# A sparse mixer on one core: latents and expansion weights split for three single-pass products, another order of the indexer, relevance on row halves

## The chip, the cores and the metric

The kernel runs on one core of one Trainium2 chip. The metric is the time of one execution on the device, in microseconds (us); the lower the better. TensorE (PE) multiplies, VectorE (DVE) and ScalarE (ACT) read its results out of PSUM and prepare its operands, GpSimd (POOL) computes the factors of the norms, and SyncE (SP) issues the transfers.

## The reference

A decoder trunk of two layers over 256 tokens of width 1024. Each layer is a half-step FFN, a token mixer, a cross-attention to a memory, and a second half-step FFN, each with a norm before and after. The mixer of the second layer is sparse, and it alone is changed:

```python
def dsa_mixer(h, w_in, cq_g, ckv_g, w_uq, w_uk, w_uv):
    cq, ckv, qi, ki, wi = jnp.split(h @ w_in, C_SPLITS, axis=-1)      # 384, 256, 512, 64, 8
    q = (rmsnorm(cq, cq_g) @ w_uq).reshape(b, s, C_HEADS, C_NOPE)     # 8 heads of 128
    ckv = rmsnorm(ckv, ckv_g)
    ...
        rel = jax.nn.relu(jnp.einsum('bthd,bsd->bths', qi[:, i0:end], ki[:, :end]))
        score = jnp.einsum('bths,bth->bts', rel, wi[:, i0:end]).astype(jnp.float32)
        _, idx = lax.top_k(jnp.where(admissible, score, -jnp.inf), kk)   # kk = 64
        ...
        p = jax.nn.softmax(jnp.where(valid[:, :, None, :], logits, -jnp.inf), -1)
```

Queries, keys and values of the 8 heads are expanded from two normalised latents (`cq`, 384 wide, and `ckv`, 256 wide). An indexer of 8 heads of 64 scores every earlier token, and attention sees only the 64 best of each query. Queries are done in two blocks of 128 tokens (t = 0 and 1).

## The kernel before

All five engines run one written-out program, each its own instructions in order; the order is written by hand in one block per engine, and semaphores tie the engines together. The sub-layers follow each other: FFN 3, FFN 4 (the FFN ahead of the sparse mixer), the mixer (number 5), cross-attention 6, FFN 7.

**Products.** Almost every weight goes through a split. SP loads a chunk of up to 128x2048 f32 into one of two `raw` buffers, ACT rounds it to fp32r in the ring `w_ring` (`hi_half`, L1656), and DVE subtracts to get the rest (`lo_half`, L2322). Activations are split in the same way, and a product is done as three single-pass matmuls, high by high, high by low and low by high (`token_terms`, `feature_terms`, `three_products`). `split_to(c)` in the ACT and DVE blocks is the place at which these engines split the chunks up to `c`; SP loads a chunk into a `raw` buffer once the low half of the chunk two before it is done. The ring has four places; a chunk is split into its place when the chunk four before it has had its last use.

The sparse mixer has chunks that are not split: `ca` and `cb` hold the expansion weights of queries (`cuq`), keys (`cuk`) and values (`cuv`) in plain f32, and `latT` holds the transposed latents in plain f32. `up` (L1298) multiplies them. A plain f32 matmul stands in the trace as two records.

**Names in the mixer.** `relevance(t, i)`: qi by ki for two heads of query block t; each of its two matmuls takes the two heads together (128 rows) against keys that are zero in one half of the rows (`kk2`, `kiT`). On ACT it is a ReLU out of PSUM, on DVE two multiply-adds into `score` (tensor `vaug`, L2756). `top_rounds`: rounds of MAX8 and MATCH_REPLACE8, eight for each block; `top_mask` makes the mask out of them. `queries(p)`, `keys(p)`: expansion for heads 2p and 2p+1. `latent_values(i, t)`: values of four heads and one block. `sparse_scores(n)`, on DVE `row_max` (mask, row maximum; its first instruction frees the PSUM bank), on ACT `exps`, on DVE `normalise` (which gives `prob_done`), on PE `prob_transposes`, on ACT `prob_copy`, on PE `sparse_values`, on ACT `output_hi`, on DVE `output_lo` (which frees the bank): this is the way of one pair of heads, units us[0] to us[3] for block 0 and us[4] to us[7] for block 1.

**PSUM banks.** Four banks rotate over results in the order of the string `SPARSE`; PE may write result n only when the engine that reads result n-4 has freed it.

## Time and profile before

| | |
|---|---|
| runs, us | 1086.25, 1084.6, 1086.06; median 1086.06 |
| profiled execution, us | 1085.41, of which the span of instructions is 1083.7 |
| granted TensorE clock, mean | 0.999 |
| PE busy | 1070.7 us, 99% of the span |
| DVE busy | 776.0 us, 72% |
| ACT busy | 564.6 us, 52% |
| chain that ended last | PE 91%, DVE 5%, ACT 2% |

Times in the rows are us from the start of the span. A row of the timeline gives start, duration, engine, line and operation; equal instructions in sequence are one row with their count, and the duration of a PE row includes the draining of its last matmul, so that the pace of PE is read from start to next start. The sparse mixer runs from 748.10 to 846.39.

### The profile page before, as it was taken

The numbers are of one execution on the slowest core, as the hardware profiler recorded it, in microseconds if no ns is written. First come the engines' busy times: TensorE is split into PE (matmuls) and PEld (weight loads), VectorE is DVE, ScalarE is ACT, GpSimd is POOL, SyncE is SP. The second block draws the span as 40 slices with busy tenths as digits, with TensorE's granted clock in tenths as the row PEclk, the third lists the DMA queues.
The fourth block names the chain that finished last, engine by engine and source line by source line (L and its number), as shares of the span: only waits on it lengthen the run. The fifth ranks groups of instructions, "written<-read, shape, count | busy, mean of one in ns | idle before, by whom it ended". The sixth has DMA issues, their size and how long they took to land.

```text
span 1083.7 us, 16043 instructions
## 1 busy us (share of the span) xinstructions
PE 1070.7 (99%) x6172; PEld 938.9 (87%) x6172; DVE 776.0 (72%) x1015; ACT 564.6 (52%) x816; POOL 67.8 (6%) x169
## 2 busy tenths in 40 slices
PE   8999999999999999999999999999999999999997
PEld 7888888998889888888888888888978989888886
DVE  5966769875886786676778667678487768676675
ACT  6534446667766753443465344345466666443442
POOL 3000010110020200000010000002100101000000
PEclk9999999999999999999999999999999999999999
DMA  8756474564144365644536564453804435745641
GB/s 322 249 192 222 165 273 132 170 205 151 50 184 152 108 247 199 228 166 183 194 108 246 209 233 159 190 194 108 272 14 143 175 117 195 252 159 191 222 165 40
DMA packets 50155, 194.59 MB, mean 180 GB/s; under 512 B 4496, under 2 KB 24480, under 8 KB 31792
## 3 DMA queue, kind: packets, MB, share of 16 engines
q1 hardware_dynamic: 48832, 189.54, 49.2%
q0 software_dynamic: 1264, 4.25, 1.4%
q8 instruction: 38, 0.62, 0.2%
q14 instruction: 21, 0.17, 0.0%
HBM read 192.73 MB, written 1.05 MB: 179 GB/s over the span
## 4 chain that ended last, share of the span: by engine, by line
PE 91%; DVE 5%; ACT 2%; issue 1%; DMA 1%; POOL 0%; SPq 0%; POOLq 0%; ACTq 0%; DVEq 0%
PE psum L960 21%; PE psum L1076 21%; PE psum L968 11%; PE psum L941 5%; PE psum L1061 3%; PE psum L1298 3%; PE psum L946 3%; PE psum L784 2%; PE psum L786 2%; PE psum L785 2%; PE psum L980 1%; PE psum L1267 1%; PE psum L1168 1%; PE psum L810 1%; PE psum L811 1%; PE psum L809 1%
## 5 line engine op out<-in xcount | busy, mean ns | idle before, releaser
L2322 DVE TENSOR_TENSOR w_ring<-raw,w_ring 128x2048 fp32r<-128x2048 f32 (+2 forms) x120 | 272.8, 2273 | 25.4 <-ACT w_ring L1656 25.1
L1656 ACT ACTIVATE w_ring<-raw 128x2048 fp32r<-128x2048 f32 x121 | 230.7, 1907 | 47.3 <-DMA raw<-in_ffn_w_gate 25.3
L2439 DVE TENSOR_REDUCE work<-psum 128x256 f32<-128x512 f32 x172 | 114.4, 687 | 175.3 <-PE psum L968 161.2
L960 PE MATMUL psum<-h_both,w_ring 128*128 128x512 f32 x1024 | 237.3, 389 | 0.0
L960 PEld LDWEIGHTS psum<-h_both,w_ring 128*128 128x128 f32 x1024 | 192.2, 188 | 39.9
L1076 PE MATMUL psum<-w_ring,g_both 128*128 128x512 f32 x936 | 220.0, 390 | 0.0
L1076 PEld LDWEIGHTS psum<-w_ring,g_both 128*128 128x128 f32 x936 | 173.2, 188 | 34.3
L1754 ACT ACTIVATE V<-work 128x512 f32<-128x512 f32 x44 | 27.9, 634 | 249.3 <-DVE work L2448 249.3
L968 PEld LDWEIGHTS psum<-h_both,w_ring 128*128 128x128 f32 x1024 | 127.1, 192 | 2.5
L968 PE MATMUL psum<-h_both,w_ring 128*128 128x256 f32 x1024 | 127.9, 283 | 0.0
L2322 DVE TENSOR_TENSOR w_ring<-QT,w_ring 128x2048 fp32r<-128x2048 f32 x40 | 91.4, 2285 | 2.4 <-ACT w_ring L1656 2.4
L1656 ACT ACTIVATE w_ring<-QT 128x2048 fp32r<-128x2048 f32 x40 | 76.2, 1905 | 1.9 <-DMA QT<-in_ffn_w_down 1.9
L1758 ACT ACTIVATE g_both<-V 128x512 fp32r<-128x512 f32 x43 | 27.2, 633 | 73.7 <-DVE V L2455 73.7
L941 PE MATMUL psum<-h_both,w_ring 128*128 128x512 f32 x240 | 57.7, 393 | 0.0
L941 PEld LDWEIGHTS psum<-h_both,w_ring 128*128 128x128 f32 x240 | 44.3, 188 | 8.8
L784 PE MATMUL psum<-h_both,w_ring 128*128 128x256 f32 x128 | 36.6, 286 | 0.9 <-DVE work L2559 0.9
L1688 ACT ACTIVATE h_both<-psum,gcol 128x128 fp32r<-128x128 f32 x112 | 30.8, 385 | 12.0 <-PE psum L1168 12.0
L786 PE MATMUL psum<-h_both,w_ring 128*128 128x256 f32 x128 | 36.2, 283 | 0.0
L785 PE MATMUL psum<-h_both,w_ring 128*128 128x256 f32 x128 | 36.2, 283 | 0.0
L1076 PE MATMUL psum<-w_ring,h_both 128*128 128x512 f32 x144 | 34.9, 396 | 0.0
L2455 DVE TENSOR_TENSOR V<-V,work 128x512 f32<-128x512 f32 x43 | 29.8, 692 | 6.3 <-ACT V L1754 2.8
L2354 DVE SCALAR_TENSOR_TENSOR h_both<-psum,gcol,h_both 128x128 fp32r<-128x128 f32 x112 | 30.3, 343 | 4.6 <-ACT h_both L1688 4.0
(336 smaller groups left out, 1560.7 us busy)
## 6 DMA issues: line engine op xcount, KB each, us to landing
raw<-in_ffn_w_gate SPq DMA_DIRECT2D x43, 1024.0 KB, 4.8
raw<-in_ffn_w_up SPq DMA_DIRECT2D x43, 1024.0 KB, 4.8
QT<-in_ffn_w_down SPq DMA_DIRECT2D x40, 1024.0 KB, 4.8
raw<-in_ab_w_in SPq DMA_DIRECT2D x7, 1024.0 KB, 5.5
gain_row<-in_norm_g POOLq DMA_DIRECT2D x8, 512.0 KB, 6.6
raw<-in_ffn_w_down SPq DMA_DIRECT2D x4, 1024.0 KB, 4.7
raw<-in_xa_wk SPq DMA_DIRECT2D x4, 1024.0 KB, 4.8
raw<-in_ab_w_out SPq DMA_DIRECT2D x4, 1024.0 KB, 5.0
```

The lines of the kernel that those rows point to most:

```text
L784: nc.tensor.matmul(o, wh, a_hi[:, k, :], start=(k == 0), stop=False)
L785: nc.tensor.matmul(o, wh, a_lo[:, k, :], start=False, stop=False)
L786: last = nc.tensor.matmul(o, wl, a_hi[:, k, :], start=False, stop=(k == KT - 1))
L941: nc.tensor.matmul(outs[j][:, :], hi[:, k, P * j:P * (j + 1)], h_both[:, k].rearrange("p a n -> p (a n)"), start=(k == 0), stop=False)
L946: last = nc.tensor.matmul(outs[j][:, 0:TOK], lo[:, k, P * j:P * (j + 1)], h_hi[:, k, :], start=False, stop=(k == KT - 1))
L960: nc.tensor.matmul(outs[-1][:, :], hi[:, k, P * j:P * (j + 1)], h_both[:, k].rearrange("p a n -> p (a n)"), start=(k == 0), stop=False)
L968: last = nc.tensor.matmul(outs[2 * n + j][:, 0:TOK], lo[:, k, P * j:P * (j + 1)], h_hi[:, k, :], start=False, stop=(k == KT - 1))
L1061: last = nc.tensor.matmul(psum[:, 2 * t + half, :], a, w[:, k, 512 * half:512 * (half + 1)], start=(first and k == 0 and a is ah and w is hi),
L1076: last = nc.tensor.matmul(psum[:, 2 * t + half, :], a, w[:, k, 512 * half:512 * (half + 1)], start=(first and k == 0 and a is ah and w is hi),
L1656: nc.scalar.activation(w_hi[:, c % RING, 0:k * n], raw_at(c)[:, 0:k * n], ACT.Copy)\
L2322: nc.vector.tensor_tensor(w_lo[:, c % RING, 0:k * n], raw_at(c)[:, 0:k * n], w_hi[:, c % RING, 0:k * n].bitcast(F32), ALU.subtract).then_i ...
L2439: nc.vector.tensor_reduce(dst[:, p % 2, TOK * j:TOK * (j + 1)], bank(name).rearrange("p (a n) -> p n a", a=2), AX.X, ALU.add)\
```

## The change

The two unsplit chunks are gone. `cuq.0`, `cuk`, `cuv` and `cuq.1` (1536, 2048, 2048 and 1536 columns) become ordinary chunks that ACT and DVE split; the latents are split too: ACT writes `lat_hi` and DVE writes `query_lo` and `key_lo` (`latent_lo`). Queries, keys and values are computed by `three_products`. The column groups of the input projection are regrouped, so that what the indexer and the queries need comes first and the latent of keys and values (`c.1`) last, in two steps, one for each block. `relevance` multiplies 64 rows by 64 rows, one head in the upper and one in the lower half of the array, each half into a PSUM bank of its own. The order of the whole mixer is written anew.

```diff
-    add("ca", *uq, uk[0], split=False)
-    add("cb", uk[1], *uv, split=False)
+    add("cuq.0", uq[0])
+    add("cuk", uk)
+    add("cuv", uv)
+    add("cuq.1", uq[1])
...
-C_COLS = [("c.0", (0, 256)), ("c.1", (256, 512)), ("c.2", (512, 640), (1152, 1224)), ("qi.0", (640, 896)),
-          ("qi.1", (896, 1152))]
+C_COLS = [("c.2", (256, 384), (1152, 1224)), ("c.0", (0, 256)), ("qi.0", (640, 896)), ("qi.1", (896, 1152)),
+          ("c.1", (384, 640))]
...
 SPARSE = """
-    rel0.0 rel0.1 rel1.0 rel1.1 ccqT.0 ccqT.1 cckvT rel0.2 rel0.3 cuq.0.0 rel1.2 rel1.3 cuk.0 cuq.0.1
-    score{0} cuk.1 cuv.0.0 score{1} cuq.1.0 pT{0} cuk.2 cuv.1.0 pv{0} score{2} pT{1} cuq.1.1 cuk.3 pv{1} cuv.0.1
+    rel0.0 rel0.1 c.1.0 rel0.2 rel0.3 c.1.1 rel1.0 rel1.1 cuq.0.0 cckvT rel1.2 rel1.3 cuq.0.1 cuk.0 cuk.1
+    cuv.0.0 cuv.1.0 score{0} score{1} cuk.2 pT{0} cuq.1.0 pv{0} score{2} pT{1} cuk.3 cuq.1.1 pv{1} cuv.0.1
     score{3} pT{2} cuv.1.1 pv{2} score{4} pT{3} pv{3} score{5} pT{4} score{6} pv{4} pT{5} score{7} pv{5} pT{6}
...
-            def relevance(t, i):
+            def relevance(t, m):
                 n = P * (t + 1)
-                up(f"rel{t}.{i}", [(slice(TOK * j, TOK * j + n),
-                                    [(qiT[:, i, P * t:P * (t + 1)], kiT[:, j, 0:n])]) for j in range(2)])
+                outs = [take(f"rel{t}.{2 * m + j}") for j in range(2)]
+                for i in range(2):
+                    for j in range(2):
+                        o = slice(64 * j, 64 * (j + 1))
+                        last = nc.tensor.matmul(outs[j][:, TOK * i:TOK * i + n], qiT[o, 2 * m + i, P * t:P * (t + 1)],
+                                                kiT[o, 0, 0:n], start=True, stop=True)
...
             def keys(p):
-                w = resident(f"cuk_{p // 2}").rearrange("p (h k) n -> p h k n", h=4)
-                up(f"cuk.{p}", [(slice(TOK * j, TOK * (j + 1)),
-                                 [(w[:, 2 * (p % 2) + j, k, :], latT[:, 3 + k, :]) for k in range(2)])
-                                for j in range(2)])
+                w = weights(C["cuk"])
+                three_products(f"cuk.{p}", [(slice(TOK * j, TOK * (j + 1)),
+                                             [([a[:, 2 * (2 * p + j) + n, :] for a in w], key_latent(n))
+                                              for n in range(2)]) for j in range(2)])
...
 # PE, order
-            relevance(0, 2)
-            relevance(0, 3)
             ready("ccqT.0")
             ready("ccqT.1")
             queries(0)
-            relevance(1, 2)
-            relevance(1, 3)
+            pe.wait_ge(lat_done, 4)
+            transposes("cckvT", [lat[:, t, QL + P * k:QL + P * (k + 1)] for k in (0, 1) for t in range(NT)])
+            relevance(1, 1)
+            queries(1)
             ready("cckvT")
             keys(0)
-            queries(1)
-            sparse_scores(0)
             keys(1)
             latent_values(0, 0)
+            latent_values(1, 0)
+            sparse_scores(0)
             sparse_scores(1)
+            keys(2)
+            prob_transposes(us[0])
             queries(2)
-            prob_transposes(us[0])
-            keys(2)
-            latent_values(1, 0)
             sparse_values(0)
             sparse_scores(2)
             prob_transposes(us[1])
+            keys(3)
             queries(3)
-            keys(3)
             sparse_values(1)
             latent_values(0, 1)
             sparse_scores(3)
...
 # DVE, order
-            for t, i in RELEVANCE:
-                relevance(t, i)
-            top_rounds(0, range(rounds))
+            latent_lo("ccqT.0", query_lo, 0, 2, 4)
+            latent_lo("ccqT.1", query_lo, 2, 1, 5)
+            split_to(C["cuq.0"])
+            relevance(0, 0)
+            relevance(0, 1)
+            split_to(C["cuk"])
+            relevance(0, 2)
+            relevance(0, 3)
+            split_to(C["cuv"])
+            latent("cckv", QL, QL + KVL)
+            top_rounds(0, range(2))
+            relevance(1, 0)
+            relevance(1, 1)
+            latent_lo("cckvT", key_lo, 0, 2, 6)
+            top_rounds(0, range(2, rounds))
             top_mask(0)
             row_max(us[0])
+            relevance(1, 2)
+            relevance(1, 3)
+            split_to(C["cuq.1"])
             top_rounds(1, range(0, 2))
+            top_rounds(1, range(2, 4))
             normalise(us[0])
             row_max(us[1])
-            top_rounds(1, range(2, 4))
+            top_rounds(1, range(4, 6))
             normalise(us[1])
-            top_rounds(1, range(4, 6))
+            top_rounds(1, range(6, rounds))
+            top_mask(1)
             row_max(us[2])
             output_lo(us[0])
-            top_rounds(1, range(6, rounds))
             normalise(us[2])
             split_to(C["co.0"])
             output_lo(us[1])
-            top_mask(1)
             row_max(us[3])
```

The place on which most depends is DVE between the row maximum of the first pair of heads and its normalised probabilities. Before, on DVE (`work<-psum,xmT` and `nmax<-work` are `row_max`, `einv` and `work<-work,einv` are `normalise`):

```order
L2559 SCALAR_TENSOR_TENSOR work<-psum,xmT 128x2x128 [waits bank_full1,dve_chain]
L2562 TENSOR_REDUCE nmax<-work 128x2 [waits bank_read1]
L2766 MAX top<-vaug 128x8
L2767 MATCH_REPLACE vaug<-top,vaug 128x256 [waits dve_chain]
L2766 MAX top<-vaug 128x8 [waits dve_chain]
L2767 MATCH_REPLACE vaug<-top,vaug 128x256 [waits dve_chain]
L2567 RECIPROCAL einv<-esum 128x2 [waits exp_done,dve_chain]
L2574 TENSOR_TENSOR work<-work,einv 128x2x128 [waits dve_chain]
```

In the changed kernel the same stretch of DVE begins so (the pair of rows MAX and MATCH_REPLACE follows four times before the RECIPROCAL, where it stood twice):

```order
L2593 SCALAR_TENSOR_TENSOR work<-psum,xmT 128x2x128 [waits bank_full1,dve_chain]
L2596 TENSOR_REDUCE nmax<-work 128x2 [waits bank_read1]
L2799 SCALAR_TENSOR_TENSOR vaug<-shared,iw,vaug 128x256 [waits bank_read2]
L2799 SCALAR_TENSOR_TENSOR vaug<-shared,iw,vaug 128x256 [waits dve_chain]
L2799 SCALAR_TENSOR_TENSOR vaug<-shared,iw,vaug 128x256 [waits bank_read3,rel_used]
L2799 SCALAR_TENSOR_TENSOR vaug<-shared,iw,vaug 128x256 [waits dve_chain]
L2356 TENSOR_TENSOR w_ring<-raw,w_ring 128x1536 [waits split_hi,rel_used]
L2809 MAX top<-vaug 128x8
L2810 MATCH_REPLACE vaug<-top,vaug 128x256 [waits dve_chain]
```

Four multiply-adds of the relevance, the low half of chunk `cuq.1` and two more rounds now stand between `row_max` and `normalise`.

The other place is PE ahead of the transposes of the first probabilities, the rows that wait for `prob_done`. Before (`KTs,QT` is `sparse_scores(1)`, the six `latT,w_raw` are `queries(2)`):

```order
L1267 MATMUL psum<-KTs,QT 128x128 [waits bank_read0,bank_read2]
L1267 MATMUL psum<-KTs,QT 128x128
L1298 MATMUL psum<-latT,w_raw 128x256 [waits bank_read1,resident_full_ca]
L1298 MATMUL psum<-latT,w_raw 128x256 x5
L1153 MATMUL psum<-ident,work 128x128 [waits bank_read2,prob_done]
L1153 MATMUL psum<-ident,work 128x128
```

In the changed kernel the end of that stretch on PE (the last three of the twelve products of `keys(2)`, the transposes, the first three of `queries(2)`):

```order
L1380 MATMUL psum<-lat_hi,w_ring 128x256
L1381 MATMUL psum<-key_lo,w_ring 128x256
L1382 MATMUL psum<-lat_hi,w_ring 128x256
L1159 MATMUL psum<-ident,work 128x128 [waits bank_read0,prob_done]
L1159 MATMUL psum<-ident,work 128x128
L1380 MATMUL psum<-lat_hi,w_ring 128x256 [waits bank_read1,split_lo]
L1381 MATMUL psum<-query_lo,w_ring 128x256
L1382 MATMUL psum<-lat_hi,w_ring 128x256
```

`queries(2)` has moved behind the transposes; between `sparse_scores(0)` and them PE now has `sparse_scores(1)` and `keys(2)` alone.

## Rows read from the trace of the kernel before

**Rows 1.** The page: its first line and part 1, busy us of PE.

```profile
span 1083.7 us, 16043 instructions
PE 1070.7 (99%) x6172; PEld 938.9 (87%) x6172; DVE 776.0 (72%) x1015; ACT 564.6 (52%) x816; POOL 67.8 (6%) x169
```

**Rows 2.** Windows of the mixer: stretch, length, busy us by engine, granted clock, DMA.

```profile
748.10:766.10 18.00, 18.00 (x152) 17.84 (x153) 12.60 (x21) 13.10 (x21) 4.56 (x8) 1.00 0.58 186
782.95:799.22 16.27, 15.97 (x75) 12.95 (x73) 12.29 (x45) 9.06 (x17) 0.00 (x0) 1.00 0.00 1
```

**Rows 3.** Timeline of PE in the sparse mixer: start, duration, line, operation.

```profile
780.77 1.25 PE L1153 MATMUL psum<-ident,lat 128*128 128x128 f32 x10
781.86 1.26 PE L1298 MATMUL psum<-krT,shared 128*128 128x128 f32 x8
782.95 2.76 PE L1298 MATMUL psum<-latT,w_raw 128*128 128x256 f32 x12
785.55 1.89 PE L1298 MATMUL psum<-krT,shared 128*128 128x256 f32 x8
787.27 4.48 PE L1298 MATMUL psum<-latT,w_raw 128*128 128x256 f32 x20
791.59 0.61 PE L1267 MATMUL psum<-KTs,QT 128*128 128x128 f32 x4
...
793.76 1.88 PE L1298 MATMUL psum<-w_raw,latT 128*128 128x512 f32 x4
795.48 0.61 PE L1267 MATMUL psum<-KTs,QT 128*128 128x128 f32 x4
796.36 2.83 PE L1298 MATMUL psum<-latT,w_raw 128*128 128x256 f32 x12 [0.27 <-DVE work L2559]
799.22 0.44 PE L1153 MATMUL psum<-ident,work 128*128 128x128 f32 x2
...
814.22 0.38 PE L1153 MATMUL psum<-ident,work 128*128 128x128 f32 x2
```

**Rows 4.** Timeline of PE in the first mixer, around `three_products`.

```profile
238.86 0.28 PE L1374 MATMUL psum<-lat_hi,w_ring 128*128 128x256 f32 x1
...
246.06 0.40 PE L1374 MATMUL psum<-w_ring,lat_hi 128*128 128x512 f32 x1
...
248.81 2.84 PE L1298 MATMUL psum<-w_raw,work 128*128 128x128 f32 x24
```

**Rows 5.** Timeline of DVE in the sparse mixer.

```profile
787.37 2.05 DVE L2756 SCALAR_TENSOR_TENSOR vaug<-shared,iw,vaug 128x256 f32<-128x256 f32 x4 [2.03 <-ACT shared L1669]
...
795.79 0.42 DVE L2559 SCALAR_TENSOR_TENSOR work<-psum,xmT 128x256 f32<-128x256 f32 x1
...
796.58 0.42 DVE L2766 MAX8 top<-vaug 128x8 f32<-128x256 f32 x1
...
798.54 0.17 DVE L2567 RECIPROCAL einv<-esum 128x2 f32<-128x2 f32 x1
...
799.08 0.42 DVE L2559 SCALAR_TENSOR_TENSOR work<-psum,xmT 128x256 f32<-128x256 f32 x1
...
807.96 2.28 DVE L2322 TENSOR_TENSOR w_ring<-raw,w_ring 128x2048 fp32r<-128x2048 f32 x1
810.16 0.42 DVE L2583 TENSOR_TENSOR h_both<-psum,h_both 128x256 fp32r<-128x256 f32 x1
...
811.27 0.42 DVE L2559 SCALAR_TENSOR_TENSOR work<-psum,xmT 128x256 f32<-128x256 f32 x1
```

**Rows 6.** Timeline of ACT: a split in the mixer.

```profile
807.33 1.90 ACT L1656 ACTIVATE w_ring<-raw 128x2048 fp32r<-128x2048 f32 x1
```

**Rows 7.** PE at the two ends of the span, and the last window's clock.

```profile
5.07 1.20 PE L903 MATMUL psum<-h_both,w_ring 128*128 128x512 f32 x2
...
1073.68 4.24 PE L1061 MATMUL psum<-w_ring,g_both 128*128 128x512 f32 x18
...
1081.50:1082.00 0.50, 0.00 (x0) 0.00 (x0) 0.00 (x0) 0.00 (x0) 0.00 (x0) 0.50 1.03 381
```

More of the change, by code:

```diff
@@ L1520, in _, with key_value_latent @@
             relevance(0, 0)
+            def key_value_latent(t):
+                hi, lo = weights(C["c.1"])
+                filled(f"c.1.{t}", token_terms(take(f"c.1.{t}")[:, 0:256], hi, lo, h_hi, h_lo, t))
+            key_value_latent(0)
+            ready("qi.1")
             relevance(0, 1)
-            filled("qi.1", feature_terms(out_[:, TOK:2 * TOK], hi, lo, h_hi, h_lo, 1))
+            key_value_latent(1)
             relevance(1, 0)
-            relevance(1, 1)
-            pe.wait_ge(lat_done, 3)
@@ new lines, in key_latent @@
+            def key_latent(n, o=slice(0, TOK)):
+                return lat_hi[:, 3 + n, o], key_lo[:, n, o]
+            def queries(p):
+                w = weights(C[f"cuq.{p // 2}"])
+                heads = [slice(HD * h, HD * (h + 1)) for h in (2 * (p % 2), 2 * (p % 2) + 1)]
+                three_products(f"cuq.{p // 2}.{p % 2}", [(slice(TOK * j, TOK * (j + 1)),
+                                                          [([a[:, n, heads[j]] for a in w], query_latent(n))
+                                                           for n in range(3)]) for j in range(2)])
@@ L1544, in latent_values @@
             def latent_values(i, t):
-                w = resident(f"cuv_{i}").rearrange("p (h k) n -> p h k n", h=4)
-                up(f"cuv.{i}.{t}", [(slice(0, 512), [(tile(latT[:, 3 + k, :], t), w[:, :, k, :]) for k in range(2)])])
+                w = [a.rearrange("p (h k) n -> p h k n", k=2)[:, 4 * i:4 * i + 4] for a in weights(C["cuv"])]
+                three_products(f"cuv.{i}.{t}", [(slice(0, 512), [(key_latent(n, slice(P * t, P * (t + 1))),
+                                                                  [a[:, :, n, :] for a in w]) for n in range(2)])])
@@ L2092, in _ @@
             us = units_of("dsa")
[L2093 to L2094 removed]
             queries(0)
+            latent_rows("cckvT", 3, 2)
             relevance(1, 2)
             relevance(1, 3)
+            queries(1)
+            split_to(C["cuq.1"])
             keys(0)
[L2099 to L2108 removed]
+            keys(1)
+            latent_values(0, 0)
+            latent_values(1, 0)
+            exps(us[0])
+            exps(us[1])
+            keys(2)
+            prob_copy(us[0])
+            queries(2)
+            split_to(C["co.0"])
             output_hi(us[0])
@@ L2744, in _, with latent @@
             dve.wait_ge(ki_done, 1)
-            for name, a, b in (("ccq", 0, QL), ("cckv", QL, QL + KVL)):
+            def latent(name, a, b):
                 for t in range(NT):
@@ L2748, in _, with latent_lo @@
                 ins.then_inc(lat_done, 1)
-            split_to(C["qi.1"] + 2)
+            split_to(C["qi.1"])
+            latent("ccq", 0, QL)
+            split_to(C["c.1"])
+            def latent_lo(name, dst, k, n, done):
+                dve.wait_ge(lat_hi_done, done)
+                first = k if dst is query_lo else 3
+                for j in range(n):
+                    ins = nc.vector.scalar_tensor_tensor(dst[:, k + j, :], bank(name)[:, TOK * j:TOK * (j + 1)],
+                                                         pcol[:, CCQ + first + j:CCQ + first + j + 1],
+                                                         lat_hi[:, first + j, :].bitcast(F32), ALU.mult, ALU.subtract)
+                ins.then_inc(freed[name][0], 1)
             def relevance(t, i):
```

120 lines of the change are left out of this document (58 added, 62 removed).

## The prediction

> **What bounds the kernel now.** I read the page first: PE is busy for 99% of a span of 1083.7 us [rows 1]. Then the windows of the sparse mixer: PE is busy for all of the 18.00 us of the input projection and for 15.97 of 16.27 us where queries, keys and values are expanded, at clock 1.00, while DVE is busy for 12.29 and ACT for 9.06 of the latter [rows 2]. Then the timeline of PE through the mixer: its rows follow each other without a gap, and the only wait above 0.2 us is 0.27 us [rows 3]. So PE sets the pace before. What is taken from PE counts in full, as long as DVE and ACT keep up; the question is whether they do once they have more to do.
>
> **What the change takes from PE.** A plain f32 matmul of 256 columns costs 4.32/10 = 0.432 us (20 records, two a matmul, from 787.27 to 791.59), one of 512 columns 1.72/2 = 0.86 us [rows 3]. The kernel has the new form already in its first mixer: 60 single products of 256 columns from 238.86 to 246.06 are 0.120 us each, 12 of 512 columns up to 248.81 are 0.229 us each [rows 4]. Three of them are 0.36 and 0.69 us.
> - Queries and keys are 24 + 16 matmuls: 40 x 0.072 = 2.9 us less. Values are 8: 8 x 0.17 = 1.4 us less.
> - The transposes for `kiT` are 2 in place of 4: 2 x 0.11 (ten took 1.09 us [rows 3]) = 0.2 us less.
> - Relevance: the pair of calls for block 0 costs 1.09 us, for block 1 1.72 us [rows 3], twice each: 5.6 us. The changed kernel issues the same 16 matmuls over the same columns, with 64 rows of the array in place of 128. No row of before shows such a matmul. If the two halves of the array take turns, it costs 5.6 us as now (full); if they overlap wholly, 2.8 us (half). The nearest rows are the full-height ones, but consecutive matmuls go to different halves and banks, so I take the middle, 4.2 us (1.4 less), and keep both ends for the range.
>
> The Trainium skill bears on this term: "TensorEngine Tiling (Array Packing)", section Key Properties, has it that tiles on different rows load weights and multiply in parallel, and that a change of tiling mode drains the array. By that page the term would be near 2.8 us, and the sum below about 1 us lower. No row here shows it.
>
> Together PE has 2.9 + 1.4 + 0.2 + 1.4 = 5.9 us less to do. The regrouping of the input projection changes nothing for PE: the same 1.00-clock 18.00 us of columns, part of them later.
>
> **What it adds elsewhere.** DVE gets four low halves, two of 2048 and two of 1536 columns. One of 2048 is 2.20 us from start to next start (807.96 to 810.16 [rows 5]); scaled by columns one of 1536 is 1.7 (an estimate), so 7.8 us in all. Five low halves of latents of 256 columns from PSUM are 0.34 to 0.42 us each like the instruction at 810.16, 1.9 us. ACT gets four high halves, about 1.8 + 1.8 + 1.4 + 1.4 = 6.4 us by [rows 6]. SP has four more loads through the two `raw` buffers; each is issued when the low half two chunks before is done, 7 us or more before PE wants the product, so I cost them at nothing. Up to `cuv` all of this falls where DVE and ACT have idle time. The last of it does not, and this is the term that decides.
>
> **The wait that appears.** A timetable from the rows. PE starts the mixer at 748.10 as before. Until the first scores it now has: 18.00 (projection), 11.54 for the two halves of qi (two stretches of 48 single products of 0.12), 0.2 (`kiT`), 1.1 (ten latent transposes), 4.2 (all of relevance), 36 products of `queries(0)` and `(1)` 4.3, 24 of `keys(0)` and `(1)` 2.9, 12 of 512 columns for values 2.75, and the scores 0.44 (791.59 to 792.03, four records). That is 45.4 us; with 0.3 us that `keys(0)` waits for `key_lo`, the scores of us[0] are done at 793.8, and readable at about 794.0. DVE has then finished the eight rounds of block 0 and waits for them.
>
> From there DVE has, in its fixed order: `row_max` 0.79 (795.79 to 796.58), four multiply-adds of 256 columns 2.05, the low half of `cuq.1` 1.7, four rounds of 0.98 (two took from 796.58 to 798.54) 3.9, `normalise` 0.6 (798.54 to 799.08, and the end of the instruction) [rows 5]. Sum 9.0: `prob_done` comes at 803.0. PE in the meantime has 0.44 for `sparse_scores(1)` and 12 x 0.12 = 1.44 for `keys(2)`, and stands still from 795.7 to 803.0, **7.3 us**. Before, the transposes that wait for it started at 799.22 [rows 3]. They are 3.8 us late. Behind them on PE stand `queries(2)` and all that follows; no engine can go around.
>
> What is late next: PE then has 0.2 (transposes), 2.16 (`queries(2)`), 0.44 + 0.44 + 0.21, 1.44 (`keys(3)`), and would start `queries(3)` at 808.0. It goes to the bank of pv of us[0], which `output_lo(us[0])` frees. DVE comes to that after `row_max(us[1])` 0.79, two rounds 1.96, `normalise` 0.54, two rounds 1.96, the mask of block 1 0.8, `row_max(us[2])` 0.79 and its own 0.42: 7.3 us after 803.0, at 810.3. That is a second wait, **2.3 us**. A third: `latent_values(1, 1)` goes to the bank of us[1]'s pv. ACT frees the way only after it has evacuated `queries(3)` (812.5, and 0.6 for 512 columns, an estimate a little above a quarter of the 1.90 of 2048 [rows 6]), split `co.1` (1.8) and written the high half of 256 (0.4, estimated alike), then DVE 0.4: 815.8, while PE would be there at 814.9: **0.9 us**. The transposes of us[3] then start at 815.8 + 1.37 + 0.44 + 0.87 = 818.5, against 814.22 before [rows 3]: 4.3 us late. From there on both kernels have the same work, PE was without gaps before, and nothing gives it back: 4.3 us is the loss at the end too. As a check by sums: waits 0.3 + 7.3 + 2.3 + 0.9 = 10.8, less the 0.27 of before, less the 5.9 saved, is 4.6.
>
> **The clock.** PE never stood still for 7 us before. At the end of the span its last matmul ends at 1077.92, and the granted clock of 1081.5 to 1082.0 is 0.50, the lower level of 1.2 GHz [rows 7]. At the start, two products of 512 columns take 1.20 us with their draining (0.5 us each from start to start), twice the 0.229 of [rows 4, 7]. So I expect the clock to fall inside the 7.3 us, and some matmuls after it at half pace. If this holds for 5 us, PE reaches `queries(3)` at 810.5 in place of 808.0, which the second wait hides; but `sparse_scores(2)` comes at 809.7, just when DVE wants it, and up to 1 us gets through. I take 0.4, bounds 0 and 1.5. The skill's "TensorE: Matmul & The Clock Gate", Part 1, has the same: an idle engine falls to half clock and regains it only after sustained work. The trace's two ends agree with it.
>
> **Sum.** The profiled execution took 1085.41 us. + 4.3 + 0.4 = **1090.1 us**. That execution is 0.65 us below the median of the runs shown, so I put the forecast between the two bases, at 1090.4.
>
> **Rivals.**
> - *The added vector work is hidden* (faster). The whole 5.9 us would be kept and the time be 1079.5. For it speaks that DVE is idle for 4 of 16.27 us at the expansion [rows 2] and more before. It decides at one point: `normalise(us[0])` would have to end by 795.7, when PE is through with `keys(2)`. Against it: 9.0 us of DVE instructions stand between the scores and it, each with a row and all on one in-order engine, and PE cannot give the scores 7 us earlier. Chance 0.05.
> - *The loss and the gain nearly cancel* (within 2 us). With relevance at half, and the two bank waits absorbed because the instructions between are shorter out of PSUM than I have them, the loss would be 4.3 - 1.0 - 2.0 = 1.3: 1086.7. The first wait alone, 7.3, is already above the 5.9. Chance 0.09.
> - *The half clock lasts.* The page on the clock gate would allow that the second and third wait keep PE at 1.2 GHz. As a mechanism of this kernel: the PE work between 803 and 818, some 12 us, would take 12 us more, less the 3.2 us of waits that it fills: 8 us or more on top, 1098. Against it: the one fall that the trace shows comes after PE has stood still from 1077.92 until past 1081 [rows 7]; the later waits are 2.3 and 0.9 us. Chance 0.06.
> - *Relevance at full price or dearer* (drains between halves): 5.6 us or more, the scores 1.4 later, and so all behind: 1091.8. Chance 0.16.
> - The forecast as summed: chance 0.64.
>
> **Numbers.** 0.2% of 1086 us, about 2.2 us, is what a measurement of this kernel tells from no change. Slower by more: 0.64 + 0.16 + 0.06 and a part of the second rival, 0.87. Within: 0.08. Faster: 0.05. The range for 8 in 10 reaches from relevance at half, no clock term and the lower base (1085.4 + 3.3, less the 1 us by which single runs differ) to the full price with 1.5 us of clock on the median: 1087.7 to 1093.3.
>
> **What would show it.** In the changed kernel's trace: `prob_transposes` of us[0] with an idle time of about 7 us before it, put down to the DVE line of `normalise`; `queries(3)` with about 2 us; products of queries at 0.12 us each; relevance from PE's starts, 2.8 or 5.6 us in all; a window below 1.00 clock right after the first wait; the end of the mixer (846.39 before) at 850.5 to 851.5, and from there the same distance to the end. I am wrong if DVE's order leaves `normalise(us[0])` earlier than 801, if the loads of `cuk` or `cuv` come late (then PE waits before 787), or if PE shows gaps of its own at the change from one form of matmul to the other.

## The result and the profile after

The changed kernel takes 1092.82 us (median of 6 runs, 1091.66 to 1095.09), the kernel before in the same session 1086.07 us (6 runs). The ratio is 1.0062, 95% interval 1.0051 to 1.0074: it is slower by 6.75 us. The forecast was 1090.4 (1087.7 to 1093.3), so the sign and the range hold, and the time is 2.4 us above the forecast. The profiled execution took 1092.22 us.

The page of the changed kernel, its first line, busy us of each engine, and the chain that ended last [rows 1 for before]:

```profile
span 1090.5 us, 16158 instructions
PE 1068.2 (98%) x6218; PEld 939.4 (86%) x6218; DVE 786.1 (72%) x1023; ACT 570.6 (52%) x821; POOL 71.7 (7%) x169
PE 85%; DVE 7%; ACT 3%; DMA 3%; issue 1%; POOL 1%; SPq 0%; POOLq 0%; DVEq 0%; ACTq 0%
```

PE has 2.5 us less busy time in a span that is 6.8 us longer: it must stand still more. To compare executions whose sub-layers start at slightly different times, I measure the mixer from the second group of input transposes, inside its start, to the first group of the next sub-layer. The timeline of PE before:

```profile
751.09 1.18 PE L1168 MATMUL psum<-ident,x_state 128*128 128x128 f32 x8
...
844.13 1.04 PE L1168 MATMUL psum<-ident,x_state 128*128 128x128 f32 x8
```

That is 93.04 us. After, the same timeline with the rows that answer to [rows 3]:

```profile
751.35 1.28 PE L1174 MATMUL psum<-ident,x_state 128*128 128x128 f32 x8
...
773.39 0.71 PE L1521 MATMUL psum<-krT,shared 64*128 64x128 f32 x8
...
777.10 0.71 PE L1521 MATMUL psum<-krT,shared 64*128 64x128 f32 x8
...
780.82 1.14 PE L1521 MATMUL psum<-krT,shared 64*128 64x256 f32 x8
...
784.87 0.66 PE L1159 MATMUL psum<-ident,lat 128*128 128x128 f32 x4 [0.57 <-DVE lat L2379]
785.46 1.13 PE L1521 MATMUL psum<-krT,shared 64*128 64x256 f32 x8
...
789.26 0.36 PE L1380 MATMUL psum<-lat_hi,w_ring 128*128 128x256 f32 x1 [0.34 <-DVE key_lo L2789]
...
794.95 1.05 PE L1273 MATMUL psum<-KTs,QT 128*128 128x128 f32 x8
...
804.82 0.69 PE L1159 MATMUL psum<-ident,work 128*128 128x128 f32 x2 [7.38 <-DVE work L2608]
...
805.94 0.41 PE L1380 MATMUL psum<-lat_hi,w_ring 128*128 128x256 f32 x1
806.15 0.41 PE L1381 MATMUL psum<-query_lo,w_ring 128*128 128x256 f32 x1
...
809.14 1.05 PE L1295 MATMUL psum<-work,V 128*128 128x128 f32 x4
810.03 0.86 PE L1273 MATMUL psum<-KTs,QT 128*128 128x128 f32 x4
...
812.26 0.28 PE L1382 MATMUL psum<-lat_hi,w_ring 128*128 128x256 f32 x1
812.65 0.35 PE L1380 MATMUL psum<-lat_hi,w_ring 128*128 128x256 f32 x1
...
818.35 0.47 PE L1380 MATMUL psum<-w_ring,lat_hi 128*128 128x512 f32 x1 [0.81 <-DVE h_both L2617]
...
821.12 0.38 PE L1159 MATMUL psum<-ident,work 128*128 128x128 f32 x2
...
850.91 1.04 PE L1174 MATMUL psum<-ident,x_state 128*128 128x128 f32 x8
```

The mixer takes 850.91 - 751.35 = 99.56 us, 6.5 more than before, and that is the whole loss but for 0.2 us. What to see: a wait of 7.38 us before the transposes of us[0], put down to `normalise` (L2608); behind it products that start 0.21 us apart in place of 0.12; only a gap of some 0.3 us before `queries(3)` (812.65); 0.81 us before `latent_values(1, 1)`; and two small waits earlier (0.57 and 0.34). From 821.12 on both kernels go at the same pace, and nothing is given back.

Four windows of the same stretch (stretch, length, busy us of PE, PEld, DVE, ACT, POOL, granted clock, DMA):

```profile
796.00:800.00 4.00, 1.43 (x12) 1.23 (x11) 3.83 (x7) 1.93 (x5) 0.00 (x0) 1.00 0.00 0
800.00:804.00 4.00, 0.00 (x0) 0.00 (x0) 3.76 (x13) 0.00 (x0) 0.00 (x0) 0.52 0.65 204
804.00:808.00 4.00, 3.19 (x15) 3.19 (x16) 3.73 (x14) 1.63 (x6) 0.00 (x0) 0.50 0.15 60
808.00:812.00 4.00, 4.00 (x26) 3.87 (x25) 3.35 (x11) 2.62 (x4) 0.00 (x0) 0.70 0.02 4
```

PE is idle, DVE is full, ACT is idle, and the clock stands at 0.50, the level of 1.2 GHz, until about 810. DVE in this stretch:

```profile
795.67 0.42 DVE L2593 SCALAR_TENSOR_TENSOR work<-psum,xmT 128x256 f32<-128x256 f32 x1 [1.78 <-PE psum L1273]
...
796.46 2.04 DVE L2799 SCALAR_TENSOR_TENSOR vaug<-shared,iw,vaug 128x256 f32<-128x256 f32 x4
798.53 1.76 DVE L2356 TENSOR_TENSOR w_ring<-raw,w_ring 128x1536 fp32r<-128x1536 f32 x1
...
804.33 0.42 DVE L2608 TENSOR_TENSOR work<-work,einv 128x256 f32<-128x256 f32 x1
```

and ACT, its split of `cuq.1` and the end of the exponentials of us[0]:

```profile
789.46 1.48 ACT L1678 ACTIVATE w_ring<-raw 128x1536 fp32r<-128x1536 f32 x1
...
797.75 0.18 ACT L1846 ACTIVATION_READ_ACCUMULATOR work<-work,nmax 128x1 f32 x1
```

From `row_max` to the end of `normalise` DVE works for 9.1 us without a gap, while the exponentials that `normalise` needs were ready by 798. DVE was idle for 1.78 us right before, with the low half of `cuq.1` already possible (ACT had split it by 790.94).

### The profile page after: what moved, and what is told of

Its sections match the earlier page's. It is cut to its first block, busy times and chain, and to the rows that moved or that the text cites. A ratio compares the mean times of both kernels' runs of the same rounds, so it can differ in the third digit from the quotient of the medians.

```text
span 1090.5 us, 16158 instructions
## 1 busy us (share of the span) xinstructions
PE 1068.2 (98%) x6218; PEld 939.4 (86%) x6218; DVE 786.1 (72%) x1023; ACT 570.6 (52%) x821; POOL 71.7 (7%) x169
## 3 DMA queue, kind: packets, MB, share of 16 engines
HBM read 192.73 MB, written 1.05 MB: 178 GB/s over the span
## 4 chain that ended last, share of the span: by engine, by line
PE 85%; DVE 7%; ACT 3%; DMA 3%; issue 1%; POOL 1%; SPq 0%; POOLq 0%; DVEq 0%; ACTq 0%
PE psum L965 21%; PE psum L1082 21%; PE psum L973 11%; PE psum L946 5%; PE psum L1067 3%; PE psum L951 3%; DVE w_ring L2356 2%; PE psum L985 1%; ACT w_ring L1678 1%; PE psum L1273 1%; PE psum L789 1%; PE psum L791 1%; PE psum L790 1%; PE psum L1295 1%; DMA raw<-in_ab_w_in 1%
## 5 line engine op out<-in xcount | busy, mean ns | idle before, releaser
L2356 DVE TENSOR_TENSOR w_ring<-raw,w_ring 128x2048 fp32r<-128x2048 f32 (+2 forms) x124 | 280.8, 2265 | 24.7 <-ACT w_ring L1678 24.1
L1678 ACT ACTIVATE w_ring<-raw 128x2048 fp32r<-128x2048 f32 (+1 forms) x125 | 237.5, 1900 | 47.7 <-DMA raw<-in_ffn_w_gate 22.0
L681 POOL TENSOR_SCALAR part<-ss,eps_in 128x1 f32<-128x1 f32 x8 | 2.5, 312 | 476.5 <-ACT V L1700 476.5
```

The lines of the kernel that those rows point to most:

```text
L1678: nc.scalar.activation(w_hi[:, c % RING, 0:k * n], raw_at(c)[:, 0:k * n], ACT.Copy)\
L2356: nc.vector.tensor_tensor(w_lo[:, c % RING, 0:k * n], raw_at(c)[:, 0:k * n], w_hi[:, c % RING, 0:k * n].bitcast(F32), ALU.subtract).then_i ...
```

## The experiments

Theory A, my prediction's: PE saves 5.9 us, and DVE's order between the first scores and `normalise(us[0])` costs more than that. Rivals: the amount of new work on DVE and ACT, or late loads, or PE's new forms cost it. All ratios are to the kernel before, run beside each kernel. Mixer times are from one profiled execution each, and so can't give their own scatter; the medians also hold what varies ahead of the mixer, which in these executions starts (its second group of input transposes) anywhere between 750.80 and 753.50.

| kernel | median us | ratio, 95% interval | mixer us | first wait us |
|---|---|---|---|---|
| before | 1086.07 | | 93.04 | |
| changed | 1092.82 | 1.0062, 1.0051 to 1.0074 | 99.56 | 7.38 |
| DVE's order (e1_order) | 1087.73 | 1.0013, 1.0004 to 1.0022 | 94.96 | 2.80 |
| normalise first (e2_first) | 1094.38 | 1.0072, 1.0059 to 1.0084 | 100.90 | 3.45 |
| wait filled (e3_filler) | 1091.33 | 1.0054, 1.0041 to 1.0067 | 99.10 | 1.63 |
| relevance on full height (e4_rows) | 1092.80 | 1.0058, 1.0045 to 1.0071 | 99.82 | 7.38 |
| contiguous loads (e5_contig) | 1091.36 | 1.0052, 1.0036 to 1.0067 | 99.84 | 7.39 |
| DVE's order, wait half filled (e7_short) | 1087.24 | 1.0013, 1.0004 to 1.0023 | 93.07 | 1.36 |
| covered (e6_cover) | 1084.28 | 0.9990, 0.9981 to 0.9999 | 91.65 | 1.08 |
| covered, full height (e8_rows) | 1085.33 | 0.9997, 0.9987 to 1.0007 | 91.96 | 0.65 |
| covered, second version (e9_cover2) | 1083.80 | 0.9980, 0.9971 to 0.9989 | 90.80 | 1.09 |

**DVE's order alone.**

```diff
-            top_rounds(0, range(2, rounds))
+            top_rounds(0, range(2, 4))
+            relevance(1, 2)
+            top_rounds(0, range(4, 8))
+            relevance(1, 3)
             top_mask(0)
+            split_to(C["cuq.1"])
             row_max(us[0])
-            relevance(1, 2)
-            relevance(1, 3)
-            split_to(C["cuq.1"])
-            top_rounds(1, range(0, 4))
+            top_rounds(1, range(0, 1))
             normalise(us[0])
             row_max(us[1])
-            top_rounds(1, range(4, 6))
+            top_rounds(1, range(1, 3))
             normalise(us[1])
-            top_rounds(1, range(6, rounds))
-            top_mask(1)
-            row_max(us[2])
+            top_rounds(1, range(3, 5))
             output_lo(us[0])
+            row_max(us[2])
...
```

> The changed kernel with DVE's order alone rewritten inside the mixer: the low half of cuq.1 and the multiply-adds of relevance(1,2) and (1,3) go ahead of row_max(us[0]), where DVE is idle for 1.78 us, normalise(us[0]) stands one round after row_max(us[0]), output_lo(us[0]) ahead of row_max(us[2]), and the rounds of block 1 are spread up to row_max(us[4]). Theory A (the loss is DVE's order, which holds prob_done back): the 7.38 us before the transposes of us[0] fall to 1 to 3 us, the clock stays at 1.00, the mixer ends 6 to 7 us earlier, and the time is 1086 us (1084.5 to 1087.5). Theory B (the loss is in the new work itself, the amount that DVE and ACT have to do, or in PE's new forms): the wait moves to other places and the time stays at 1092 to 1093. Theory C (late loads of cuk and cuv set it): the same, 1092 or more.

Measured: 1087.73 us, 5.1 below the changed kernel, and the mixer 4.6 us shorter, though not one instruction of arithmetic was taken out. So the order, not the amount of work, made most of the loss; theories B and C fall as its main cause. But it is 1.7 us above what I expected, and 0.2 us above the upper end of my range. PE's timeline shows why:

```profile
802.18 0.44 PE L1159 MATMUL psum<-ident,work 128*128 128x128 f32 x2 [2.80 <-DVE work L2608]
802.37 0.36 PE L1380 MATMUL psum<-lat_hi,w_ring 128*128 128x256 f32 x1
...
802.69 0.41 PE L1382 MATMUL psum<-lat_hi,w_ring 128*128 128x256 f32 x1
802.89 0.42 PE L1380 MATMUL psum<-lat_hi,w_ring 128*128 128x256 f32 x1
```

The first wait is still 2.80 us, and after it the products go from 0.12 to 0.21 us apart, until 805.9: `queries(2)` takes 1.5 us more than at full clock. I had said that the clock would stay at 1.00. It did not: it stands at 1.00 from 802.40 to 802.60, when PE is at work again, and at 0.50 from 802.80 to 803.00. What is left of the wait is DVE's order too: the low half of `cuq.1` (797.94, 1.76 us) still stood ahead of `row_max(us[0])`, which began at 799.61. Its scores were there 2.0 us earlier, if they take as long to be read as in the changed kernel (794.95 to 795.67).

**`normalise(us[0])` ahead of the rounds, nothing else.**

```diff
             split_to(C["cuq.1"])
-            top_rounds(1, range(0, 2))
-            top_rounds(1, range(2, 4))
             normalise(us[0])
             row_max(us[1])
-            top_rounds(1, range(4, 6))
+            top_rounds(1, range(0, 6))
             normalise(us[1])
```

> The changed kernel with normalise(us[0]) and row_max(us[1]) moved ahead of the four rounds, nothing else. Theory A as a chain (all that stands on DVE up to row_max(us[2]) must be done, wherever normalise stands): the wait before the transposes of us[0] falls from 7.38 to about 3.5 us, and waits of together 3 to 4 us come up before the transposes of us[1] and queries(3); the time falls by the clock's share at most, 1091 to 1093. Rival (the first wait counts for itself, as my prediction summed it): 3.9 us less, about 1089.

Measured: 1094.38 us, not faster at all, and above the 1091 to 1093 that I gave it. The waits on PE:

```profile
801.49 0.44 PE L1159 MATMUL psum<-ident,work 128*128 128x128 f32 x2 [3.45 <-DVE work L2608]
808.70 0.44 PE L1159 MATMUL psum<-ident,work 128*128 128x128 f32 x2 [2.07 <-DVE work L2608]
812.66 0.55 PE L1380 MATMUL psum<-lat_hi,w_ring 128*128 128x256 f32 x1 [1.53 <-DVE h_both L2617]
```

The long wait halves, and two others come up, before the transposes of us[1] and before `queries(3)`. What counts is all that DVE has to do up to `row_max(us[2])` and `output_lo(us[0])`; a single wait is only where it shows. The mixer is even 1.3 us longer: with three waits in a row the granted clock stays low over five windows of 4 us from 800 (0.86, 0.71, 0.72, 0.50, 0.93), where the changed kernel had three. The rival of 1089 falls. That the clock makes up all of these 1.3 us was not tested.

**The wait filled with work on PE.**

```diff
-                for cols, terms in tiles:
+                for cols, terms in tiles * times:
...
-                                              for n in range(2)]) for j in range(2)])
+                                              for n in range(2)]) for j in range(2)], 5 if p == 2 else 1)
```

> The changed kernel, but PE does the twelve products of keys(2) five times into the same bank, which fills 5.8 of the 7.38 us wait with work and leaves the results as they are. Theory A1 (the half clock delays queries(2), ACT's split of co.0 behind it and so output_lo(us[0]) and queries(3)): no window below 1.00, queries(2) at 0.12 us a product, and the mixer ends 0.9 us earlier (0.6 to 1.3): 1091.9. Rival A2 (the second wait hides all of the half clock): no difference, 1092.8. Rival A3 (all of the half clock counts): 2.4 us less, 1090.4.

Measured: 1091.33 us, mixer 99.10, 0.46 us less than changed. The granted clock is 1.00 in every window from 796 to 820. From the transposes of us[0] to those of us[3] it takes 15.73 us (804.35 to 820.08), against 16.30 in the changed kernel (804.82 to 821.12), and the wait that the half clock had filled comes out:

```profile
804.35 0.44 PE L1159 MATMUL psum<-ident,work 128*128 128x128 f32 x2 [1.63 <-DVE work L2608]
811.61 0.36 PE L1380 MATMUL psum<-lat_hi,w_ring 128*128 128x256 f32 x1 [1.64 <-DVE h_both L2617]
```

So of some 2.7 us that the slow matmuls take more (`queries(2)` 3.99 for 2.16, values 0.89 for 0.44, scores 0.69 for 0.44, and the transposes), only 0.5 to 0.6 us reach the end. That is just below the lower end that I gave A1 (0.6 to 1.3) and not the nothing of A2; A3 (2.4 us) falls. The medians (1091.33 and 1092.82, from two sessions) have ratios with overlapping intervals and do not part A1 from A2.

**Relevance on the full height.**

```diff
-                        o = slice(64 * j, 64 * (j + 1))
-                        last = nc.tensor.matmul(..., qiT[o, 2 * m + i, ...], kiT[o, 0, 0:n], ...)
+                        last = nc.tensor.matmul(..., qiT[:, 2 * m + i, ...], kiT[:, j, 0:n], ...)
```

> The changed kernel with relevance on the full height again (the keys padded with zeros as before, kiT of four transposes, a memset on DVE), in the changed order. Theory A (PE sets the time at which the scores of us[0] are ready): relevance takes 5.6 in place of 3.4 us, less what it covers of the wait of 0.57 us before cckvT, plus 0.2 for the transposes: the scores and all behind are 1.9 to 2.4 us later, 1094.7 to 1095.2. Rival (DVE sets it, so that the row halves bring nothing): 1092.8. Rival (a change of form costs PE as much as the halves save): 1092.8 too, with relevance at about 5 us in the changed kernel's rows, which they don't show.

Measured: 1092.80 us, the same as changed; the mixer is 0.26 us longer. The 1.9 to 2.4 us of theory A were wrong twice. First, the price. The rows of this kernel:

```profile
783.28 1.89 PE L1520 MATMUL psum<-krT,shared 128*128 128x256 f32 x8
784.82 0.47 PE L1380 MATMUL psum<-lat_hi,w_ring 128*128 128x256 f32 x1
```

From its start to the next instruction a call of block 1 takes 1.54 us here and 1.06 in the changed kernel. That is not the whole, for the products behind it lose time too. Counted from the start of a call to that of the last product behind it, less 0.12 us for each product between, the four calls are 0.74, 0.75, 1.16 and 1.15 us in halves, with 0.09 or 0.10 lost ahead of each, and 0.88, 0.89, 1.72 and 1.72 on the full height, with next to nothing ahead: 4.2 against 5.2. (For the first: 773.39 to 776.89, 23 products further, is 3.50, less 23 x 0.12.) The halves save 1.0 us, with the two transposes 1.3. Second, of this only 0.3 arrives, because the waits of 0.57 and 0.34 us in the changed kernel disappear when PE comes later.

**Contiguous loads.** The two arrays are laid out so that a partition's part of `cuk` and `cuv` is one run.

```diff
+    elif name in ('c_w_uk', 'c_w_uv'):
+        a = a.reshape(a.shape[0], a.shape[1], 2, P, a.shape[3]).transpose(0, 3, 1, 2, 4)
```

> The changed kernel with c_w_uk and c_w_uv laid out in memory so that each partition's part of a chunk is one run of 8 KB in place of sixteen of 512 bytes; nothing else. Theory A (late loads make the wait before the transposes of cckvT): the two loads take 4.5 to 5 us from issue to landing, like the other loads of 1 MB, in place of 6.6 and 7.0; ACT's wait of 0.80 us before the split of cuk goes, and so does the wait of 0.57 us before the transposes of cckvT; the mixer, from the input transposes in it to those behind it, takes 99.0 us in place of 99.56. Rival (what DVE has to do sets the time of the key latent, with or without the loads): the wait of 0.57 stays, and the mixer with it.

The DMA issues of both kernels, the changed one first (median us from issue to landing; for the load in runs of 512 bytes the view gives the KB of a run, 0.5, not those of the whole):

```profile
raw<-in_c_w_uk SPq DMA_DIRECT2D x1, 0.5 KB, 6.6
raw<-in_c_w_uv SPq DMA_DIRECT2D x1, 0.5 KB, 7.0
```

```profile
raw<-in_c_w_uk SPq DMA_DIRECT2D x1, 1024.0 KB, 4.7
raw<-in_c_w_uv SPq DMA_DIRECT2D x1, 1024.0 KB, 4.8
```

As expected 2 us faster, and the wait before `cckvT` is gone: from the first relevance to the first scores it takes 20.79 us (774.60 to 795.39) in place of 21.56. The mixer as a whole does not show it in this execution: an earlier load of `c_w_in` landed later (the two loads took 6.1 us in the middle against 5.3), ACT waited for it for 3.28 us, and PE stood still for 0.98 us ahead of `qi.1`. That also brought PE to `cckvT` some 1.2 us later, which by itself would hide a wait of 0.57 us. The three kernels with these loads further down settle it: their PE is not late (first relevance at 772.88 to 773.23, against 773.39 in the changed kernel), and none has a wait before `cckvT` or for these loads. So the local effect is shown; in the total it is not told apart from nothing (ratio 1.0052 against 1.0062, intervals overlapping).

**The shorter wait, half filled.** The first of these kernels (DVE's order), with `keys(2)` done twice.

> The kernel of the first run (DVE's order alone rewritten), and PE does the products of keys(2) twice into the same bank: 1.44 us of work in the wait of 2.80 us that stood there. The clock had been below 1.00 after it (0.84 and 0.74 in two windows of 4 us). Theory A1 (a wait of 2.8 us is enough to lose the clock, one of 1.4 is not): no window below 1.00, and the mixer takes 94.0 us in place of 94.96. Rival (the half clock there was hidden by other waits): 94.9 as before.

Measured: the granted clock is 1.00 in all windows, and the mixer is 93.07, 1.9 us below 94.96, though PE does 1.44 us more. 0.3 us of this is a shorter wait before `cckvT`. The median fell only from 1087.73 to 1087.24 with the same ratio to before, so that the gain of 1 us and more stands in the two traces alone.

**The order that covers the softmax.** PE's part of the edit is shown. Four things differ from the changed kernel at once: the contiguous loads, PE's order, ACT's with it, and DVE's, which is not quite that of e1_order: `relevance(1, 3)` and `row_max(us[1])` stand between `row_max(us[0])` and `normalise(us[0])`, and the low half of `cuq.1` is done ahead of the last round of block 0. What each is worth was not measured apart.

```diff
             latent_values(0, 0)
-            latent_values(1, 0)
             sparse_scores(0)
+            latent_values(1, 0)
             sparse_scores(1)
             keys(2)
+            latent_values(0, 1)
             prob_transposes(us[0])
             queries(2)
...
             sparse_values(1)
-            latent_values(0, 1)
             sparse_scores(3)
+            latent_values(1, 1)
             prob_transposes(us[2])
-            latent_values(1, 1)
```

> Arithmetic, chunks and row halves of the changed kernel with the contiguous loads of the run before, DVE's order rewritten as in the first run, and PE's order (with ACT's and the banks') changed so that the time of us[0]'s softmax is covered: latent_values(1, 0) behind sparse_scores(0), latent_values(0, 1) behind keys(2), latent_values(1, 1) behind sparse_scores(3). Theory A (the new arithmetic is worth 5 us on PE, and only waits took it away): PE waits 2 to 4 us in all in the mixer, the clock stays at 1.00, the mixer takes 90 to 91.5 us against 93.04 before, and the time is 1083.5 us (1082.5 to 1085), below the kernel before. Rival (DVE has too much to do between the scores and row_max(us[4]), in any order): the waits go elsewhere and sum to over 6 us, and the time is not below 1086.

Measured: 1084.28 us, ratio 0.9990 (0.9981 to 0.9999), as expected; the mixer, 91.65, is 0.15 us above what I gave it. Its waits are 3.5 us in all, the longest of them is new, and the clock is 1.00:

```profile
811.50 0.68 PE L1293 MATMUL psum<-work,V 128*128 128x128 f32 x4 [1.32 <-ACT work L1689]
```

**The same with relevance on the full height.** The edit is that of the kernel with full height above.

> The kernel of the run e6_cover with relevance on the full height again (keys padded with zeros, kiT of four transposes). By the rows of the two kernels run so far relevance with the changes of form around it takes 5.4 us on the full height and 4.45 in halves, and two transposes take 0.27. Theory A (in the changed order the halves bring little only because waits behind them give way, and in a kernel without these waits they count): 1.0 to 1.3 us more than that kernel. Rival (they bring nothing anywhere): within 0.3 us of it.

Measured: mixer 91.96, 0.31 us more; by the traces theory A missed. The waits give way again: 0.32 us before `keys(0)` is gone, and 1.08 before the transposes of us[0] becomes 0.65. The medians are 1.05 us apart (1085.33 and 1084.28), which would fit theory A, but the intervals overlap, and they cannot decide between 0.3 and 1.

**The second version of the cover.** `latent_values(1, 1)` goes back behind the transposes of us[2], and `prob_copy(us[2])` ahead of `exps(us[3])` on ACT. DVE's order differs in some places too: the low half of `cuq.1` now stands behind `row_max(us[0])`, `relevance(1, 3)` behind `row_max(us[1])`.

> The kernel of the run e6_cover with latent_values(1, 1) back behind the transposes of us[2], prob_copy(us[2]) ahead of exps(us[3]) on ACT, and small moves in DVE's order. In e6_cover PE waited 1.32 us before the values of us[2], because the copy of their probabilities had nothing to hide behind. Theory A (that wait was the order's): it falls to 0.5 us or less, the mixer takes 90.5 to 91.2 us in place of 91.65, and the time is 1083.5 us (1082.5 to 1084.5). Rival (DVE is full from the scores to row_max(us[4]) and any cover only moves the wait): 91.5 to 92 us again.

Measured: 1083.80 us, ratio 0.9980 (0.9971 to 0.9989): faster than both kernels. The wait before the values of us[2] is 0.30 us and the mixer 90.80.

```profile
798.64 0.44 PE L1157 MATMUL psum<-ident,work 128*128 128x128 f32 x2 [1.09 <-DVE work L2606]
...
810.32 0.68 PE L1293 MATMUL psum<-work,V 128*128 128x128 f32 x4 [0.30 <-DVE h_both L2615]
```

The first wait, 1.09 us, is still in part order. The exponentials of us[0] are complete at 797.12, but DVE is at `relevance(1, 3)` then, and `normalise` begins at 797.96:

```profile
796.93 0.99 DVE L2797 SCALAR_TENSOR_TENSOR vaug<-shared,iw,vaug 128x256 f32<-128x256 f32 x2
797.96 0.17 DVE L2599 RECIPROCAL einv<-esum 128x2 f32<-128x2 f32 x1
```

In the same chain ACT spends 1.28 us (from 794.94) on loading its table ahead of the first exponential. Neither was tried out.

**Each matmul of relevance three times,** in halves and on the full height, to part the price of a matmul from that of the change of form.

```diff
-                for i in range(2):
+                for i in 3 * (0,) + 3 * (1,):
...
```

> The changed kernel with each matmul of relevance issued three times into the same place, so that what a matmul on half of the rows costs stands apart from what a change of form costs. Theory A (the halves overlap in part): by the changed kernel's rows, 1.06 us for a call of block 1 (four matmuls, eight records) and 0.64 for one of block 0, so the calls take 3.2 and 1.9 us. Theory B (they overlap wholly, and the rest is the cost of the change of form): every further repetition of block 1 costs 0.86 us, half of the 1.72 of the kernel before, and the call takes 2.8 us; block 0 1.6 us. Theory C (they do not overlap; the first figure only looks short because the next instruction shows later): 1.72 us for a repetition, 4.5 us for the call.

> The same threefold issue in the kernel e4_rows, relevance on the full height. A call of block 1 took 1.54 us there by its row and 1.82 with what the next products lose; a call of block 0 0.81 and 0.88. If a matmul on the full height costs what it did in the kernel before (0.43 us for 256 columns, 0.22 to 0.27 for 128), the calls take 5.0 to 5.2 and 2.6 to 3.0 us.

Each of the two kernels ran once (1096.17 and 1102.28 us); only their traces are used. PE in the two, halves first, with a call of block 0 and one of block 1:

```profile
778.05 1.61 PE L1522 MATMUL psum<-krT,shared 64*128 64x128 f32 x24
779.59 0.39 PE L814 MATMUL psum<-w_ring,h_both 128*128 128x256 f32 x1
...
782.66 2.86 PE L1522 MATMUL psum<-krT,shared 64*128 64x256 f32 x24
785.45 0.39 PE L1380 MATMUL psum<-lat_hi,w_ring 128*128 128x256 f32 x1
```

```profile
784.28 5.34 PE L1521 MATMUL psum<-krT,shared 128*128 128x256 f32 x24
789.27 0.47 PE L1380 MATMUL psum<-lat_hi,w_ring 128*128 128x256 f32 x1
```

A call of block 1 takes 2.79 us in halves, 1.73 more than once: 0.865 for each further issue. On the full height it takes 4.99 us, 3.45 more than once: 1.73 for each. The halves cost exactly half, as theory B has it: two of them run in the time of one matmul on the full height. That they do so side by side is the reading; a matmul on one half with none on the other was not run, so that 64 rows alone take half the time is not excluded. What a single call costs beyond this, with the 0.09 ahead of it, is 1.25 - 0.865 = 0.39 us for block 1 and 0.83 - 0.445 = 0.39 for block 0 (a further issue is 0.445 there: 1.54 us for the call of 778.05, 0.65 once). On the full height there is nothing beyond (1.72 against 1.73), in calls that stand between the same products; so I put the 0.4 us down to the change to halves and back.

## Why the prediction was right, and where it was short

The mechanism held: PE saved less than it then lost to a wait for `normalise(us[0])`, and DVE's order made that wait. Signs by which I would see it are there (7.38 us before the transposes of us[0], products at 0.12 us, a window below 1.00), except that the mixer ended at 853.17, not between 850.5 and 851.5, and `queries(3)` waited for 0.3 us, not for 2. Two of my three signs of being wrong came up as well, both small: the load of `cuk` came late, and PE has gaps where the form changes.

- **PE bound before, less on PE after: right, and the sum nearly so.** The waits in the rows sum to 9.1 us, but they are counted from the end of a drained matmul. From start to start, less the usual pace, PE loses 0.73, 0.49, 7.55, 0.27 and 1.06 us, 10.1 in all, and 2.7 by half pace: 99.56 - 12.8 = 86.8 us of work, against 93.04 - 0.6 = 92.4 before. So about 5.7 us were saved, forecast 5.9 (an estimate from these rows, good to some tenths). Products are 0.12 us apart as read from the first mixer.
- **Relevance: right in size by luck.** I took the middle between "the halves take turns" and "they overlap" (4.2 us), and it came to 4.2, but not by a middle of the two. The halves come at half the price, 2.6 us in all, and each of the four calls loses 0.39 us beside. The Trainium skill has both in "TensorEngine Tiling (Array Packing)", Key Properties: tiles work in parallel, and a change of mode drains the array; the runs agree, with 0.865 against 1.73 us and 0.39 us a call. My reading that the page gives 2.8 us left out the drains, whose size it does not state: 1.6 us in four calls, more than half of the 2.8 us that the halves give.
- **Loads at nothing: wrong by 0.6 to 0.7 us.** The 6.6 us that `cuk` took to land held ACT's split of it back by 0.80 us, and the key latent with it: the wait of 0.57 us, which is gone in the covered kernels with faster loads.
- **The first wait: right in place, cause and length (7.3 forecast, 7.38 measured).** The 9.0 us of DVE were 9.1. What was off is its start: `row_max(us[0])` begins at 795.67, not 794.0. PE started the mixer 0.37 us later in this execution; the other 1.3 us are in the stretch until the end of the first scores. It was put at 45.4 us and 0.3 for `keys(0)`, and takes 46.9 (748.47 to 795.39): 0.7 is the wait before `cckvT`, 0.5 that before `keys(0)`, and 45.7 are PE's work, 0.3 more than summed, most likely for the changes of form. So the step of the prediction that was mis-sized is the loads at nothing in this sum.
- **The second wait: 2.3 forecast, 0.3 shown.** It is there as soon as the clock stays up (1.64 in the filled kernel); in the changed kernel the half clock fills it, as the paragraph on the clock had it.
- **The third wait: 0.9 forecast, 0.81 measured.**
- **The clock: 0.4 forecast, 0.5 to 0.6 measured.** It fell inside the wait, as forecast. "TensorE: Matmul & The Clock Gate", Part 1, in the Trainium skill says that an idle engine falls to half clock and comes back after sustained work; the windows at 0.52, with PE idle, and at 0.50 and 0.70, with PE back at work, agree.
- **The sum.** 4.3 + 0.4 for the mixer, measured 6.5: 1.3 from the late scores, 0.2 from the clock, and 0.3 that I can't assign. The rival *hidden vector work* named the right point, `normalise(us[0])` by the time PE is through with its cover: the second cover gets within 1.09 us of it, by the order of three engines and the layout of two loads, and is faster than before. It keeps 2.2 of some 5.7 us that PE saves in the mixer. Most of the rest is in its waits, 2.5 us as the rows list them and 3.5 from start to start.

Whether the halves would bring their 1 us in a kernel without waits before `keys(0)` and us[0] stays open: both pairs of kernels had such waits.

## What to carry to other kernels

When work moves from the bounding engine to one that has idle time, look not at its busy share but at the chain between a result and the answer that the first engine waits for: here 7.7 us of work that could have stood elsewhere were in it. A new order on DVE alone brought 5.1 of the 6.8 us of loss back; with a new order on PE and ACT and two loads in longer runs, and no arithmetic taken out, it became a gain of 2.3 us. Moving one instruction forward is not enough when everything behind it has a date too: give DVE's list in the order of those dates, and put the bounding engine's own free work (here products of values that nobody waits for) into the latency that is left. Small array tiles pay more in long runs: a call of four lost some 0.4 us to the change there and back, which left 0.5 us of gain for block 1 (1.25 against 1.72 us) and next to nothing for block 0 (0.83 against 0.88).

## What the runs showed of the hardware that was not expected

- A shorter wait lost the clock too. After PE had stood still for 2.80 us, the products were 0.21 us apart from 802.69 to 805.9, beginning only after the wait had ended. After waits of 1.36, and of 1.63 and 1.64 us, no window was below 1.00; but where waits of 2.07 and 1.53 us followed one of 3.45 (e2_first), five windows in a row were.
- Matmuls on 64 of 128 rows, alternating between the halves, ran at 0.865 us for four of 256 columns against 1.73 on the full height, in plain f32 (e10_thrice_half, e11_thrice_full).
- A load of 1 MB in runs of 512 bytes landed after 6.6 and 7.0 us, in one run per partition after 4.7 and 4.8.
